# Down projections of a two-layer encoder on one Trainium2 core: nine Strassen pairs and four ordinary row groups in place of eight and six, their weights split by ScalarE and VectorE

## The reference

```python
def conv_ffn(x, w_up, conv_w, conv_b, w_down):
    hdn = x @ w_up                                   # 1024 -> 5632
    hdn = causal_dwconv(hdn, conv_w, conv_b)         # 3 taps along the tokens
    val, gate = jnp.split(hdn, [D_FF], axis=-1)
    return (jax.nn.gelu(gate) * val) @ w_down        # 2816 -> 1024

ff = conv_ffn(x, ...)
x = layer_norm(ALPHA * x + ff, ln2_g[i], ln2_b[i])
gate = jax.nn.sigmoid(x @ ple_gate_w[i] + ple_gate_b[i])
x = x + gate * (p[i] @ ple_w[i])                     # p[i]: 512 x 256
```

## Time and profile before

| | us |
|---|---|
| median of 3 runs (lowest, highest) | 1244.78 (1243.01, 1246.21) |
| the profiled execution, device time | 1244.86 |
| its span, first to last instruction | 1243.1 |
| down projection, layer 0: folds, from the first fold matmul | 500.7 to 577.3 |
| layer 0: first ordinary matmul to first gate matmul | 577.27 to 629.74 |
| layer 1: the same two stretches | 1065.4 to 1142.8, 1142.84 to 1195.49 |

### The profile page before, as it was taken

The page is one execution under the profiler, slowest core; times in us unless marked ns, Lnnn a source line. Parts: engine busy times, 40 slices in busy tenths (PEclk is TensorE's granted clock), DMA queues, the critical chain, the costliest instruction groups (busy, mean ns, idle before and its releaser), DMA issues.

```text
span 1243.1 us, 17094 instructions
## 1 busy us (share of the span) xinstructions
PE 1230.7 (99%) x5733; PEld 1000.9 (81%) x5733; DVE 733.5 (59%) x1100; ACT 431.6 (35%) x723; POOL 743.9 (60%) x990
## 2 busy tenths in 40 slices
PE   9999999999999999999999999999999999999998
PEld 6887777788888888888788778888888888788787
DVE  6555556565545644899744374374644444899742
ACT  4445444222212223562244484112222222563141
POOL 7554467719877775303677547929887776201673
PEclk9999999999999999999999999999999999999999
DMA  5212232303332232864243222313332233674321
GB/s 199 70 68 68 68 116 88 119 6 114 101 101 87 99 124 79 268 196 146 85 170 102 84 69 85 120 51 102 101 101 92 94 101 118 204 222 148 104 93 60
DMA packets 74194, 137.44 MB, mean 111 GB/s; under 512 B 4272, under 2 KB 52976, under 8 KB 73632
## 3 DMA queue, kind: packets, MB, share of 16 engines
q1 hardware_dynamic: 73088, 134.23, 33.1%
q10 hardware_dynamic: 1056, 2.58, 0.6%
HBM read 134.60 MB, written 2.20 MB: 110 GB/s over the span
## 4 chain that ended last, share of the span: by engine, by line
PE 90%; DVE 3%; POOL 2%; issue 1%; POOLq 1%; ACT 1%; DMA 1%; DVEq 0%; ACTq 0%; SPq 0%
PE bank L560 19%; PE bank L562 19%; PE bank L561 19%; PE bank L579 3%; PE bank L916 3%; PE bank L918 3%; PE bank L917 3%; PE bank L581 3%; PE bank L580 3%; PE bank L854 2%; PE bank L861 2%; PE bank L856 2%; PE bank L675 1%; PE bank L662 1%; POOL w_lo L546 1%
## 5 line engine op out<-in xcount | busy, mean ns | idle before, releaser
L546 POOL TENSOR_TENSOR w_lo<-stage,w_hi 128x256 fp32r<-128x256 f32 x656 | 483.4, 768 | 24.2 <-issue 1.5
L540 POOL TENSOR_SCALAR w_hi<-stage 128x1024 fp32r<-128x1024 f32 x164 | 179.2, 1093 | 224.9 <-DMA stage<-w_down 113.2
L560 PE MATMUL bank<-x_hi,w_hi 128*128 128x512 f32 (+1 forms) x712 | 275.7, 387 | 0.0
L562 PE MATMUL bank<-x_hi,w_lo 128*128 128x512 f32 (+1 forms) x712 | 275.4, 387 | 0.0
L561 PE MATMUL bank<-x_lo,w_hi 128*128 128x512 f32 (+1 forms) x712 | 275.4, 387 | 0.0
L1317 DVE SCALAR_TENSOR_TENSOR tmp<-bank,cols,tmp 128x511 f32<-128x511 f32 x88 | 65.5, 745 | 204.0 <-ACT tmp L1751 204.0
L1751 ACT ACTIVATE tmp<-bank,cols 128x512 f32<-128x512 f32 x88 | 63.9, 778 | 294.9 <-PE bank L562 273.3
L561 PEld LDWEIGHTS bank<-x_lo,w_hi 128*128 128x128 f32 x712 | 133.7, 188 | 27.2
L560 PEld LDWEIGHTS bank<-x_hi,w_hi 128*128 128x128 f32 x712 | 133.7, 188 | 27.0
L562 PEld LDWEIGHTS bank<-x_hi,w_lo 128*128 128x128 f32 x712 | 133.7, 188 | 27.0
L560 PE MATMUL bank<-in_hi,w_hi 128*128 128x512 f32 x312 | 130.0, 417 | 0.0
(11 more groups left out here) (226 smaller groups left out, 2114.9 us busy)
## 6 DMA issues: line engine op xcount, KB each, us to landing
stage<-w_square SPq DMA_DIRECT2D x163, 512.0 KB, 3.3
stage<-w_down SPq DMA_DIRECT2D x56, 512.0 KB, 4.1
stage_far<-w_down SPq DMA_DIRECT2D x20, 512.0 KB, 4.5
rows<-norm_rows SPq DMA_DIRECT2D x4, 1024.0 KB, 5.5
outT<-x SPq DMA_DIRECT2D x7, 256.0 KB, 2.0
x<-xT SPq DMA_DIRECT2D x3, 512.0 KB, 6.8
p_in<-pT ACTq DMA_DIRECT2D x2, 512.0 KB, 3.3
w_ai<-w_lru SPq DMA_DIRECT2D x1, 1024.0 KB, 7.8
```

The lines of the kernel that those rows point to most:

```text
L540: whole = pool.tensor_scalar(high[:, s, :], stage[:, s, :], 1.0, 0.0, ALU.mult, ALU.add)
L546: piece = pool.tensor_tensor(low[:, s, to], stage[:, s, to], high[:, s, to].bitcast(F32), ALU.subtract)
L560: pe.matmul(out, w_hi[:, s, c:c + P], m_hi, start=first, stop=False)
L562: return pe.matmul(out, w_lo[:, s, c:c + P], m_hi, start=False, stop=last)
```

## The change

`PRE` goes from 8 to 9, so nine pairs (18 row groups) are folded and `REST = 4` ordinary groups remain. `OWN` becomes all units of the down projection (36 + 4 = 40): ACT and DVE split the ordinary units too, POOL splits none of them and forms nine first sums. In DVE's queue the low parts of units 38 and 39 come before the `kept` folds, one on either side of the last `h_low`. The embedding input is fetched by ACT in the second pass, its high part is copied between units 37 and 38, and its parts lie in the space of the folded activations, not in `tmp`, so ACT no longer waits for `kept_read`. The turn of (0, 1) moves from (2, 4) to (3, 0). The embedding and gate units use other slots, and their first four loads wait for `fold_low`.

```diff
-PRE = 8
+PRE = 9
 FOLD = 2 * PRE
 REST = FT - FOLD
 FOLD_UNITS = 4 * PRE
-OWN = FOLD_UNITS + 2
+OWN = FOLD_UNITS + REST
...
-        a = [tmp_at]
+        shared = at[0]
+        a = [shared]
         p_hi = place("p_hi", [P, PLE_TILES, SEQ], F32R, a)
...
-                for r in range(OWN, len(ph.slots)):
-                    s = ph.slots[r]
-                    last = [m for m in range(OWN) if fold_stage(m) == s][-1]
-                    sp.wait_ge(fold_low, layer * OWN + last + 1)
-                    sp.dma_start(stage[:, s, :].rearrange("p (a n) -> p a n", a=4),
-                                 rest_source(layer, r)).then_inc(unit_loaded[s], 16)
...
-                        sp.wait_ge(unit_split, ph.stage_free(i, r))
+                        if name.startswith("ple") or (name.startswith("gate") and r < 2):
+                            sp.wait_ge(fold_low, layer * OWN + fold_last(s) + 1)
+                        else:
+                            sp.wait_ge(unit_split, ph.stage_free(i, r))
...
-                beside = {(2, 2): (0, 0), (2, 4): (0, 1)}
+                beside = {(2, 2): (0, 0), (3, 0): (0, 1)}
...
-                unit_low(layer, FOLD_UNITS + 1)
+                unit_low(layer, rest + 1)
...
                 folded_in.then_inc(bank_folded, 1)
+                unit_low(layer, rest + 2)
                 h_low(layer, last, 1)
+                unit_low(layer, rest + 3)
                 dve.wait_ge(bank_kept, layer * 3 + 3)
...
-                unit_top(layer, FOLD_UNITS)
-                unit_top(layer, FOLD_UNITS + 1)
+                    if i == 3:
+                        act.wait_ge(unit_used, phases[f"up{layer}"].done(last, 3))
+                        act.dma_start(p_in[:], pT[layer]).then_inc(p_loaded, 16)
+                for r in range(FOLD_UNITS, OWN):
+                    if r == FOLD_UNITS + 2:
+                        embedding_input(layer)
+                    unit_top(layer, r)
...
-                act.wait_ge(kept_read, layer + 1)
+                act.wait_ge(unit_used, phases[f"down{layer}"].done(0, FOLD + 3))
```

More of the change, by code:

```diff
@@ L129, in plan @@
     ring, apart = [3, 0, 1, 2], [7, 4, 5, 6]
+    turned = [1, 2, 3, 0]
     want = [("qkv", [0, 1, 2], PAIRS)]
@@ L134, in plan @@
         want += [(f"out{layer}", ring + apart, 1), (f"up{layer}", ring, 2 * FT // 4),
-                 (f"down{layer}", ring * ((FOLD_UNITS + REST) // 4) + ring[:REST % 4], 1),
-                 (f"ple{layer}", ring[REST % 4:], 1),
-                 (f"gate{layer}", ring * 2, 1)]
+                 (f"down{layer}", ring * (OWN // 4), 1), (f"ple{layer}", ring[:2], 1),
+                 (f"gate{layer}", turned * 2, 1)]
     phases, first, filled = {}, 0, [0] * SLOTS
@@ L161, in fold_stage, with fold_last @@
     return [3, 0, 1, 2][r] if r < 4 else [3, 0, 4, 5, 1, 2][(r - 4) % FOLD_STAGES]
+def fold_last(s):
+    return [n for n in range(OWN) if fold_stage(n) == s][-1]
 def fold_before(r):
@@ L213, in hybrid_trunk_kernel @@
         p_in = place("p_in", [P, PLE_TILES, SEQ], F32, [x_hi_at])
-        a = [tmp_at]
+        shared = at[0]
+        a = [shared]
         p_hi = place("p_hi", [P, PLE_TILES, SEQ], F32R, a)
         p_lo = place("p_lo", [P, PLE_TILES, SEQ], F32R, a)
-        shared = at[0]
         assert x_hi_at % ROW == 0 and tmp_at % ROW == 0 and shared % ROW == 0
@@ L291, in hybrid_trunk_kernel @@
             sem(n) for n in ("fold_sides_ready", "first_summed", "fold_low"))
-        product_done, bank_kept, bank_folded, kept_read = (
-            sem(n) for n in ("product_done", "bank_kept", "bank_folded", "kept_read"))
+        product_done, bank_kept, bank_folded = (
+            sem(n) for n in ("product_done", "bank_kept", "bank_folded"))
         unit_split = sem("unit_split")
@@ L973, in down_phase @@
                 for k in range(REST):
-                    if k % 2 == 0 and FOLD_UNITS + k // 2 < OWN:
+                    if k % 2 == 0:
                         fold_ready(layer, FOLD_UNITS + k // 2)
-                    elif k % 2 == 0:
-                        unit_ready(ph, 0, FOLD_UNITS + k // 2)
                     pe.wait_ge(h_lo_ready, layer * REST + k + 1)
@@ L993, in down_phase @@
                         if t == 0 and k % 2 == 0:
-                            unit_ready(ph, 0, FOLD_UNITS + REST // 2 + k // 2)
+                            fold_ready(layer, FOLD_UNITS + REST // 2 + k // 2)
                         mm = down_step(layer, 1, t, k)
@@ L1441, in fold_down @@
                     unit_low(layer, r + 1)
-                unit_low(layer, FOLD_UNITS)
+                rest = FOLD_UNITS
+                unit_low(layer, rest)
                 dve.wait_ge(product_done, layer * 3 + 2)
@@ L1469, in fold_down @@
                 for tau in range(2):
-                    kept = block_fold(tau, 0, kept_d[tau], False, True)
-                kept.then_inc(kept_read, 1)
+                    block_fold(tau, 0, kept_d[tau], False, True)
                 dve.drain()
+                embed(layer)
             def decay_magnitudes():
@@ L1532, in rest_of_layer @@
                 fold_down(layer)
-                embed(layer)
                 layer_norm(2 * layer + 1, layer)
@@ L1835, in conv_ffn @@
                     unit_top(layer, FOLD + 2 * i + 1)
-                unit_top(layer, FOLD_UNITS)
-                unit_top(layer, FOLD_UNITS + 1)
+                    if i == 3:
[5 more added lines that the diff above has]
+                    unit_top(layer, r)
             def embedding_input(layer):
-                act.wait_ge(unit_used, phases[f"up{layer}"].done(2 * FT // 4 - 1, 3))
-                act.dma_start(p_in[:], pT[layer]).then_inc(p_loaded, 16)
                 act.wait_ge(p_loaded, 16 * (layer + 1))
-                act.wait_ge(kept_read, layer + 1)
+                act.wait_ge(unit_used, phases[f"down{layer}"].done(0, FOLD + 3))
                 for k in range(PLE_TILES):
@@ L1916, in rest_of_layer @@
                 conv_ffn(layer)
-                embedding_input(layer)
                 layer_norm_out(2 * layer + 1, layer)
```

## The result

The changed kernel takes **1261.34 us** (median of 4 runs, 1260.3 to 1261.54), the kernel before 1243.89 us beside it (4 runs, 1240.6 to 1246.21): ratio 1.0136, 95% interval 1.0115 to 1.0157. It is slower by 17 us. The forecast was 1260 us. The profiled spans differ by 16.7 us (1259.8 against 1243.1).

The account below looks back on a forecast made before the run. PE looks full at 99%, but DVE's queue was taken to bound the down projection's tail. Per layer, folds +9.6 and tail -2.1 gave +7.5; two layers +15.1 on 1244.86 gave 1260 us, range 1250 to 1267.

Parts of the forecast that it names:

- What bounds the kernel: In the down projection's tail DVE is nearly as full as PE, busy 44.85 of 52.4 us, hidden by its overall 59%.
- Folds +9.6: One more folded pair adds 42 matmuls before the first ordinary matmul: +9.6 us a layer, nothing charged for DVE.
- PE at the turn, E+17.8: PE reaches the turn of tile (0, 0) after 78 ordinary matmuls, 17.8 us after the first one starts (E).
- T at E+28.3: DVE scales tile (0, 0) 28.3 us after the first ordinary matmul starts: 25.6 work, +2.3 low parts, +0.4 POOL; ends 24.2, 30.
- The term for POOL: Net slowing of DVE's queue before tile (0, 0) is scaled, from POOL's embedding splits beside it: +0.4 us.
- The rule against my sign: DVE instructions with two SBUF inputs contend with POOL's SBUF reads; removing POOL's splits should speed DVE's queue, -4.4 us at best.
- From T to the gate, 22.2: From scaling tile (0, 0) to the first gate matmul: DVE's 18.2, PE's 3.0, half clock +1.0, 22.2 us.
- The sum: Per layer, folds +9.6 and tail -2.1 give +7.5 us; two layers +15.1, hence 1260 us.
- A: Rival: PE stays the bound with DVE scaling tile (0, 0) before PE arrives; tail 37.0 us, kernel 1233 us; chance 0.05.
- the turning point of E+21.8: Scaling tile (0, 0) 21.8 us after the first ordinary matmul, tail 43.0 us, is where loss turns to gain.
- B: Rival: POOL's going frees DVE's queue, tile (0, 0) scaled at 24.2, clock costs nothing; tail 45.4, 1250 us; chance 0.12.
- C: Rival: clock stays low behind the turn while DVE feeds PE, costing 3.4 us; tail 54.6, 1268 us; chance 0.15.

Follow-up runs that it names:

- e1: Changed kernel with DVE leaving out the six folds of the kept banks into the residual (output incomplete): 1247.02 us, ratio 1.0026 to the kernel before.
- e2: Changed kernel with POOL again splitting the last two ordinary units, 38 and 39: 1255.85 us, ratio 1.0094 to the kernel before.
- e3: Changed kernel with POOL's split of the first embedding unit held until the embedding input's low parts are there: 1250.02 us, ratio 1.0047 to the kernel before.
- e4: Eight pairs as in the kernel before, but all down-projection units split by ACT and DVE, none by POOL: 1237.34 us, ratio 0.9945 to the kernel before.
- e6: Changed kernel with 44 extra matmuls a layer filling PE's wait before the turn of (0, 0): 1258.48 us, ratio 1.0122 to the kernel before.
- e7: Changed kernel; POOL scales two residual tiles, adds four of six kept folds, splits embedding units afterwards; first two turns behind half 1: 1242.71 us, ratio 0.9998.
- e5: Changed kernel with the turns of (0, 0) and (0, 1) moved behind half 1's last matmul: 1258.17 us, ratio 1.0123 to the kernel before.
- e8: Eight pairs, ACT and DVE splitting all down-projection units, POOL adding four of six kept folds and splitting embedding units late: 1234.61 us, ratio 0.9934.

## Why the prediction was right, step by step

- *What bounds the kernel.* Right: in the tail it is DVE's queue, which the 59% of the page hides. e1, e2 and e3 show it in three doses: T earlier by 6.6, 2.7 and 5.6 us a layer made the kernel 14.3, 5.5 and 11.3 us shorter.
- *Folds +9.6.* Measured +9.4 in layer 0 (76.57 to 85.99) and +8.3 in layer 1 (77.39 to 85.68). The layer 1 of before holds a wait of PE for a low part of a fold unit, 0.94 us at 1082.87, which doesn't come back in the changed kernel. Charging nothing for DVE in the folds was right: the changed kernel has no wait of PE there. Why the old wait went wasn't tried.
- *PE at the turn, E+17.8.* Measured E+18.9 (ready after 78 matmuls and the 0.77 us wait for h_low, which had been put at up to 1 us).
- *T at E+28.3.* Measured E+29.4 in both layers, within the ends of 24.2 and 30. The term for POOL was mis-sized: +0.4 was charged against the mean of before, it was +1.5 (29.4 less 25.6 and 2.3). The two low parts lost 1.3 and h_low 0.5, about as said. Won back were 0.3 on unit 37 and 0.8 on the kept folds and the embedding input (597.23 to 606.16, 8.9 us against 9.7) where 1.7 in all was counted on: POOL's splits, put at some 5 us each, took 6.7 and 6.1, and the second ran until 605.1, past nearly all of the kept folds; and both layers now resemble layer 0 of before (26.25 us of work), not the mean with layer 1.
- *The rule against my sign.* DVE's instructions with two SBUF inputs were slowed by POOL's work here, by 5.6 us a layer (e3), and the gain that it promises was real but lay in e3 and e4, not in the change, which put POOL's embedding splits in the place of the ones taken away.
- *From T to the gate, 22.2.* Measured 22.9 and 22.5. In layer 0 DVE took 19.5 us to scale tile (3, 0), and 17.9 in e6 without the half clock, where 18.2 was forecast; PE's end behind that took 3.4 for 3.0; the clock's share is 1.6 and not 1.0. Part of that agreement is luck: the 18.2 still held a wait of 0.38 us for ACT at 609.04.
- *The sum.* +15.1 forecast, +16.7 in the spans: tails -0.2 and -0.7 instead of -2.1 each, folds +9.4 and +8.3 instead of +9.6. The tails shrank by less than forecast and the folds cost less, so the total is nearer than its terms: the mechanism was right, and that 1260 hit 1261.34 within 1.4 us is in part luck.
- *Rivals.* A said that PE works through the tail in 37.0 us once DVE is at T before it. In e7, with the first two turns behind half 1, it was (E+21.7 against PE's E+22.0), and the tail took 42.6: the time came to that of before, as the turning point of E+21.8 said, and not to 1233. B's T of 24.2 is near what e3 measured (23.8), with 1250.02 us against the 1250 worked out; e3 lies 0.4 below this lower end, because the eight instructions were put at 0.7 us each, their duration, and not at 0.60, the distance of their starts (they took 5.1 us and not 5.6). But e3 is not the changed kernel: what B supposed of the change itself, that POOL gets out of DVE's way, did not happen. C's clock cost of 3.4 us did not come (1.6), nor did the clock stay low in the changed kernel while DVE fed PE. In e5, where less work is left for PE, it did (mean 0.65 from 616 to 630), and the gate came no later for it.

## What to carry to other kernels

When one engine looks full and another 59% busy, read both over the stretch that the change shortens: matmuls saved there are worth nothing if the other engine's queue reaches the end of it no sooner, and matmuls added ahead of it are paid in full. Moving work between GpSimd and VectorE is worth trying with its timing, not only its amount: here the same GpSimd splits cost 11 us beside VectorE's SBUF work and slowed nothing beside its PSUM work. The two parts of this change had opposite signs, and only taking them apart found the faster kernel: with eight pairs the reassignment gains 6 us, and the ninth pair costs 24 us on top of it as it stands, 12.7 with POOL's splits delayed (e3) and 8.1 between the two kernels with the shortest queues (e7, e8). A part's price depends on what the other parts leave on the fuller engine, so give it with the kernel that it was measured in.

## What the runs showed of the hardware

- VectorE beside GpSimd: a 128x512 instruction with both inputs in SBUF takes 0.60 us from start to start alone (e3) and 1.14 to 1.46 beside GpSimd's splits (changed kernel), one of 1024 columns 1.13 and 1.7 to 1.9; GpSimd's four 128x256 pieces go from 2.82 to 4.43 and 5.48. The loss is on both sides at once. Folds that read PSUM take 3.83 us for six with GpSimd at work beside them (before) and without (changed kernel).
- Granted clock: a TensorE wait of 10.6 us left it at half (1.2 GHz) for 5.4 us of work behind the wait, a wait of 2.3 us before the change for about 3.3 us. A wait more than four times as long lengthened the slow stretch by 2 us only, and filling the wait with matmuls kept the full clock (1.00 in e6, 0.80 without them). Behind e5's wait of 6.6 us the mean was 0.65 from 616 to 630, and the gate still came at E+50.7, as at the full clock of e6: even at that clock TensorE kept up with VectorE there.
